# Hybrid decoder layer on one core: another order of the q, k, v preparation, the recurrence's norm in decode unit 0, query weights loaded later

## The reference

```python
h = rms_norm(x, norm1_g) * (1.0 + scale1) + shift1     # shift, scale, gate: silu(c) @ w_ada + b_ada
z = h @ w_in
x_lru, g_lru, q_lat, kv_lat, k_rope = split(z)          # 512, 512, 256, 128, 32 columns
x_conv = causal_dwconv(x_lru, ...)
hs = rg_lru(x_conv, ...)                                # h_t = a_t * h_(t-1) + u_t over the tokens
lru_out = hs * gelu(g_lru)
q = rms_norm(q_lat, q_lora_norm_g) @ w_uq               # 8 heads of 64 + 32
q_nope, q_rope = rms_norm(q[..., :64]), apply_rope(rms_norm(q[..., 64:]))
kv_lat = rms_norm(kv_lat, kv_lora_norm_g)
k_rope = apply_rope(rms_norm(k_rope, k_rope_norm_g))
attn = attend(q_nope, q_rope, kv_lat, k_rope)           # keys: rms_norm of kv_lat @ w_ukv, per head; values
mixed = concat([rms_norm(lru_out, lru_out_norm_g), rms_norm(attn, mla_out_norm_g)]) @ w_o
x = x + gate1 * mixed
x = x + gate2 * mlp(rms_norm(x, norm2_g) * (1.0 + scale2) + shift2)
```

## Time and profile before

| | us |
|---|---|
| median of 3 runs | 1013.28 |
| lowest and highest | 1012.67, 1016.78 |
| the profiled execution | 1014.83 |
| its span on the core | 1013.0 |

### The profile page before, as it was taken

The page is one execution under the profiler, slowest core; times in us unless marked ns, Lnnn a source line. Parts: engine busy times, 40 slices in busy tenths (PEclk is TensorE's granted clock), DMA queues, the critical chain, the costliest instruction groups (busy, mean ns, idle before and its releaser), DMA issues.

```text
span 1013.0 us, 20471 instructions
## 1 busy us (share of the span) xinstructions
PE 944.9 (93%) x7908; PEld 880.4 (87%) x7908; DVE 659.4 (65%) x1259; ACT 528.5 (52%) x1183; POOL 183.0 (18%) x186
## 2 busy tenths in 40 slices
PE   6599798889999999999988988999999999999997
PEld 3388675679999999999987988999999999999997
DVE  2694267538889879879783557777777777732321
ACT  2323553458898898988973333444434443321210
POOL 0021120322333343333210131000101001000000
PEclk9699899879999999999996998999999999999999
DMA  9965740600122022022101430333333331653202
GB/s 339 333 193 170 229 160 7 231 1 2 28 100 84 22 104 85 22 85 93 55 19 45 134 69 27 99 83 83 83 106 101 83 83 41 171 154 79 61 4 85
DMA packets 106289, 100.13 MB, mean 99 GB/s; under 512 B 7119, under 2 KB 94943, under 8 KB 104126
## 3 DMA queue, kind: packets, MB, share of 16 engines
q1 hardware_dynamic: 102422, 77.91, 26.4%
q0 software_dynamic: 3456, 20.97, 5.9%
q10 hardware_dynamic: 340, 0.27, 0.1%
HBM read 96.41 MB, written 2.94 MB: 98 GB/s over the span
## 4 chain that ended last, share of the span: by engine, by line
PE 85%; DVE 7%; ACT 3%; DMA 3%; issue 1%; SPq 0%; DVEq 0%; ACTq 0%
PE ps L874 50%; PE ps L1242 19%; PE ps L869 7%; DMA RW<-w_ada 3%; PE ps L900 2%; PE ps L1149 2%; PE ps L1200 1%; PE ps L1237 1%; PE ps L1175 1%; PE ps L1035 1%; DVE RB L1913 1%; DVE normed_low L1814 1%; DVE RB L1788 0%; DVE RB L2235 0%; PE ps L1100 0%
## 5 line engine op out<-in xcount | busy, mean ns | idle before, releaser
L874 PE MATMUL ps<-normed_high,up_weights_high 128*128 128x260 f32 x704 | 142.7, 284 | 3.4 <-DVE normed_low L1814 3.2
L874 PE MATMUL ps<-normed_high,up_weights_low 128*128 128x260 f32 x704 | 142.3, 284 | 0.0
L874 PE MATMUL ps<-normed_low,up_weights_high 128*128 128x260 f32 x704 | 142.1, 284 | 0.0
L1654 ACT ACTIVATE up_weights_high<-RW 128x1024 fp32r<-128x1024 f32 x44 | 46.6, 1061 | 137.2 <-PE ps L874 133.3
L1242 PE MATMUL ps<-key_weights_high,latents_high 128*128 128x260 f32 x528 | 117.4, 304 | 0.7 <-ACT RB L1596 0.6
L832 POOL TENSOR_TENSOR latents_low<-RB,latents_high 128x512 fp32r<-128x512 f32 (+1 forms) x72 | 86.2, 1198 | 174.8 <-ACT latents_high L1549 174.8
L874 PEld LDWEIGHTS ps<-normed_high,up_weights_high 128*128 128x128 f32 x704 | 109.2, 190 | 4.1 <-issue 3.3
L874 PEld LDWEIGHTS ps<-normed_high,up_weights_low 128*128 128x128 f32 x704 | 109.0, 189 | 0.0
L874 PEld LDWEIGHTS ps<-normed_low,up_weights_high 128*128 128x128 f32 x704 | 108.8, 189 | 0.0
L1242 PE MATMUL ps<-key_weights_low,latents_high 128*128 128x260 f32 x528 | 107.2, 285 | 0.0
L1242 PE MATMUL ps<-key_weights_high,latents_low 128*128 128x260 f32 x528 | 107.2, 285 | 0.0
(11 more groups left out here) (314 smaller groups left out, 2178.2 us busy)
## 6 DMA issues: line engine op xcount, KB each, us to landing
RW<-w_ada SPq DMA_DIRECT2D x24, 1024.0 KB, 8.6
RW<-w_up SPq DMA_DIRECT2D x44, 512.0 KB, 5.0
RW<-w_down SPq DMA_DIRECT2D x8, 1408.0 KB, 7.2
RW<-w_in SPq DMA_DIRECT2D x11, 512.0 KB, 8.0
RB<-w_o SPq DMA_DIRECT2D x8, 512.0 KB, 4.1
RB<-x_prompt SPq DMA_DIRECT2D x2, 1024.0 KB, 12.6
o_y_p<-RB SPq DMA_DIRECT2D x4, 512.0 KB
cst<-consts SPq DMA_DIRECT2D x1, 845.0 KB, 11.2
```

Source lines behind the costliest of these rows:

```text
L874: last = mm(ps[j % 4][rows[0]:rows[1], h, 0:H], lhsT, src[:, h * H:(h + 1) * H], start=start, stop=stop)
L1654: A(wuH[:, KT * g:KT * g + KT, :], wup[:, c, KT * g:KT * g + KT, :], ACT.Copy).then_inc(s_whi, 1)
```

## The change

Nothing is computed differently; the order changes, and with it the slots and some buffers.

- **TensorE.** kv0 and kv1 go ahead of w9, kv2 and kv3 behind it (before: behind w10 and w11). qst and qa go behind w10. The last w_ada chunk and c5 go ahead of w11. The norm sum of the recurrence (nlru) leaves the stretch: it is done in decode unit 0 behind key tile 5, as a job of the key slots.
- **ACT.** The recurrence's two Ln go ahead of the two latent norms, its Exp ahead of the gate branch. Squares and norms follow TensorE's order; query tiles go in pairs. The high part of the key weights is made here (before: DVE). The recurrence's squares and norm go into unit 0, behind key tiles 1 and 6.
- **DVE.** The recurrence goes ahead of the third group of modulation columns, the copy of modulation rows 4 and the rope key's norm. The copy of modulation rows 5 goes behind query tiles 2 and 3. The multiplication with the recurrence's norm (4 operations) goes into groups 2 and 3 of unit 0.
- **POOL.** It makes the low part of the key weights. Before its first latents_low it also waits for the ten output stores, because that buffer now lies on otok and lout, from which they are made.
- **SP.** The query and value weights are issued one projection chunk and one w_ada chunk later.

The diff, cut:

```diff
-            + ["gr", "wt", "w6", "r4", "nq", "w7", "c3", "nkv", "w8", "kr0", "w9", "r5", "qs", "kr1", "q0", "q1", "w10", "c4",
-               "q2", "q3", "kv0", "kv1", "w11"])
-PREP_ORDER = ["c5", "qst", "kv2", "kv3"] + [f"l{n}" for n in range(7)] + ["qa", "spread", "nlru"]
+            + ["gr", "wt", "w6", "r4", "nq", "w7", "c3", "nkv", "w8", "kr0", "kv0", "kv1", "w9", "r5", "kv2", "kv3", "qs", "kr1",
+               "q0", "q1", "w10", "c4", "qst", "qa", "q2", "q3", "c5", "w11"])
+PREP_ORDER = [f"l{n}" for n in range(7)] + ["spread"]
 
...
+J_NLRU = 2 + LRU_AT + 1
+KEY_JOBS = UNIT * NS + 1
...
-        latL = nc.alloc_sbuf_tensor_at("latents_low", [P, 3, 4 * P], FR, offset=rb_at + 4 * 11120)
+        latL = nc.alloc_sbuf_tensor_at("latents_low", [P, 3, 4 * P], FR, offset=behind_at)
...
-                if n == 8:
+                if n == 9:
                     query_weights()
...
+            pool.wait_ge(s_wkn, 16)
+            pool.wait_ge(s_kw, 2)
+            for e in range(2):
+                nc.gpsimd.tensor_tensor(kwL[:, e, :, 0:4 * NOPE], wk2, kwH[:, e, :, 0:4 * NOPE].bitcast(F32), ALU.subtract).then_inc(s_kw, 1)
...
+            pool.wait_ge(s_out, 16 * 10)
...
+            pe.wait_ge(s_kvn, 1)
+            pe.wait_ge(s_wq, 32)
+            keys_and_values(0)
+            keys_and_values(1)
+            w_in(9)
+            later_chunk(12)
+            later_chunk(13)
+
+            keys_and_values(2)
+            keys_and_values(3)
...
-            queries(2)
-            queries(3)
-            pe.wait_ge(s_kvn, 1)
-            keys_and_values(0)
-            keys_and_values(1)
-            w_in(11)
-            later_chunk(15)
-            mod_columns(5)
...
+            claim(pe, J_QA)
+            pe.wait_ge(s_qg, 4)
+            pe.wait_ge(psum_free[J_WT % 4], free_value(J_WT))
+            for h in range(HEADS):
+                last = mm(flat(J_QA)[:, NS * h:NS * h + NS], keyT[0:NOPE, P * h:P * h + P], gq8[:, h, :], start=True, stop=True)
+            last.then_inc(psum_full[J_QA % 4], 1)
...
+            queries(2)
+            queries(3)
+            later_chunk(15)
+            mod_columns(5)
+            w_in(11)
...
+            def lru_sum():
+
+                kclaim(J_NLRU)
+                for k in range(LT):
+                    pe.wait_ge(s_sq, KT + 4 + k + 1)
+                    for h in range(2):
+                        last = mm(kslot(J_NLRU)[:, h, 0:H], ones, lru_sq[:, k, h * H:(h + 1) * H], start=(k == 0), stop=(k == LT - 1))
+                last.then_inc(key_full[J_NLRU % 3], 1)
...
+            act.wait_ge(s_tiny, 1)
+            st.did(A(sq[:, 4:8, :], TA[:, :, :], ACT.Ln, bias=1.0))
+            st.seq(A(TA[:, :, :], TA[:, :, :], ACT.Ln))
+            act.sem_inc(s_lru, 1)
...
+            act.wait_ge(s_tiny, 2)
+            A(TA[:, :, :], TA[:, :, :], ACT.Exp, scale=0.5).then_inc(s_lru, 1)
...
+                        if u == 0 and (g, n) == (0, 1):
+                            lru_squares()
+                        if u == 0 and (g, n) == (1, 2):
+                            lru_rstd()
...
+            dve.wait_ge(s_lru, 1)
+            V.scalar_tensor_tensor(TA[:, :, :], TA[:, :, :], LN2, sq[:, 4:8, :], ADD, SUB).then_inc(s_tiny, 1)
...
+            mod_columns(3)
+            mod_rows(4)
+            dve.wait_ge(s_rs, 4)
+            R = (NOPE, QK)
+            kr = krT[NOPE:QK, :]
+            V.scalar_tensor_tensor(kr, kr, pr("gk", 0, 1, R), sq[NOPE:QK, 2, :], MUL, MUL).then_inc(s_kr, 1)
...
+            for a in range(2, 4):
+                prep_sums(5 + a, query_sq[a % 2], HEADS)
+            prep_query_tile(2)
+            prep_query_tile(3)
+            mod_rows(5)
+            dve.wait_ge(s_kr, 2)
+            dve.wait_ge(s_qtok, 4)
+            V.tensor_copy(headk[NOPE:QK, :], krT[NOPE:QK, 0:NP]).then_inc(s_krk, 1)
+            mod_columns(5)
...
+                        if u == 0 and g in (2, 3) and n % 2 == 1:
+                            lru_normed(2 * g + n // 2 - 4)
```

184 lines of the change are left out of this document (73 added, 111 removed).

## The result

The changed kernel takes 1028.18 us (median of 4 runs, 1027.41 to 1028.27), the kernel before 1014.15 (4 runs, 1012.67 to 1016.78): a ratio of 1.0134, with a 95% interval of 1.0111 to 1.0157. It is slower by 1.3%. I had forecast 1013.9, with a range of 1008.5 to 1019.7. The profiled execution took 1027.41 with a span of 1025.6, against 1014.83 and 1013.0 before, so these two executions differ by 12.6 us.

A forecast was written before the change was run, and what follows sets the result against it. TensorE, 85% of the span, was taken as the bound. Unit 0's first key product 3.7 us early and unit 0 4.3 longer gave +0.6 on the median 1013.28: 1013.9 us, range 1008.5 to 1019.7.

The forecast's parts named there:

- The 6.85 us and their half clock: TensorE's wait before the second modulation chunk goes, with the slow clock behind it; next projection chunk 9.0 us early.
- The waits at kr0 and c5: New TensorE waits for DVE: 7.9 us at the key-rope norm, 6.4 at the last modulation columns, each with 2.0 half clock.
- The waits at kr1 and qa: TensorE waits 1.6 us for DVE to finish keys 2, and 1.2 for the turned sample queries before the eight products.
- the first gain: Next projection chunk starts 9.0 us early at 112.9; nearly all handed back at the key-rope norm.
- preparation in the new order: TensorE's jobs from the key-rope norm on: queries 2 and 3 end at 178.5, the last projection chunk at 194.5.
- from there to K: Last projection chunk to unit 0's first key product: fetch 195.1, new-token row 209.1, that product 211.2, 3.7 us early.
- Rival (b): Stores pass only after the whole fetch drains: first key product of unit 0 at 217.0, time 1019.7 us; chance 0.18.
- the norm in unit 0: Decode unit 0 grows 4.3 us: products 2.8, DVE's multiplications 1.5, ACT's squares 0.
- Rival (a): Stores share with the fetch, row lands with the latents: unit 0's first key product at 209.3, time 1011.2 us; chance 0.20.
- the weight split: Key-weight copies move to ACT, subtractions to POOL; DVE loses 2.2 us of work; effect 0, up to 1.

The follow-up runs named there:

- the kernel of four repairs: Changed kernel with modulation columns ahead of scans, modulation rows ahead of query tiles 2 and 3, norm in fetch wait, unit-1 fetch behind new-token rows: 1004.90 us.

## Why the prediction was wrong

**Right.** The 6.85 us and their half clock go. The waits at kr0 and c5 come, each with its cause: undoing one order each brought back 10.2 and 5.3 us, forecast 9.9 and 8.4. The second is less for the most part because waits of 1.57 and 0.49 remained in the same place. The waits at kr1 and qa came at 1.60 and 1.18, forecast 1.6 and 1.2. That most of the first gain would be handed back was right, and it was the smaller half of the matter.

**Wrong, step "preparation in the new order" (6.0 us at the first fetch).** Two terms took TensorE to be at full clock where it was not. Behind the wait at kr0, which ended 0.7 late, the granted clock averaged 0.53 from 136.7 to 145, so keys 0 and 1 (1.7 each in the sum) came out at half clock for longer than the 2.0 us counted, and the chunk behind them began 2.4 late. (How long it lasts is in part chance: from kr0 to the next w_ada chunk eleven profiles with the same code and wait took 12.8 to 14.2 us, this one 14.2.) And queries 2 and 3 took 8.4, not 5.2: I had counted the wait of 1.2 at qa and not what stands at half clock behind it. The run with qa behind the tiles shows that term alone. The wait at c5 was 0.9 longer, as long as one addition of DVE was held up at 188.43 (last section). With 0.3 more for qa, c5 began 6.8 late; the last projection chunk was then 1.2 shorter than its sum, and the fetch began 0.5 later behind it: 6.0.

**Wrong, step "from there to K" (5.7 us).** The sum took stores and fetches as served in the order of issue, so that the row would land 14 behind the first fetch. It was used 19.2 behind. What the runs show in place of that order is sharing by packets: from 205 to 218 us 858 packets of the stores passed beside 710 of the fetch, and the row, last of its queue, came when both were through. In the kernel with the row ahead of the eight stores it was there within 7.6 us of its issue, in the middle of the fetch. I read the earlier trace rows the wrong way: no packet of the stores passed before 199, but the first of them was issued only at 195.65, and in the changed kernel too nearly 2 us lie between the issue at 203.21 and the first packets. The size of the fetch was wrong as well: it moved 5.24 MB for both units, and the sum has 3.1.

Rival (b) had K 21.9 behind the first fetch, and 21.8 was measured. That is luck as far as its reason goes: the stores didn't pass only when the fetch had drained, three quarters of their packets passed before.

**Mis-sized, the norm in unit 0 (4.3 forecast, 6.9 in the profile, 7.8 by the run with the norm outside).** The products were taken at 2.8 and the multiplications at 1.5, near enough to 3.3 and 1.7. What was left out is what goes on around them, 2 us: ACT has nothing to do while TensorE multiplies for the norm, and its Ln and Exp then stand ahead of the copies that TensorE needs, which shows as a wait of 0.72, and 1.2 is open; and the squares, set at 0, cost 0.9.

**What it did not see.** The frame of the sum, "K is set by the fetch and the row", was right, but it priced the new order only up to the fetch. Before, 23 us of TensorE's work (kv2, kv3, the transposes for output, qa, the norm) lay behind the last projection chunk and covered the fetch. The change moved kv2, kv3 and qa ahead of that chunk and the norm behind K, and left 8.4 us, so that TensorE waits 7.31 and 6.05 for transfers. The kernel with the norm in that wait has unit 0 7.8 us shorter and K no later; the kernel with the last chunk ahead of queries 2 and 3 gives cover back, loses the wait at c5 and is 14 us faster.

Rival (a), that the stores share with the fetch, had the reason nearly right and the time wrong (K 14.2 behind the first fetch): it let the row land as soon as the latents, and left out that more than a thousand small packets stand ahead of the row in its queue. The Trainium skill, DMA: Bandwidth & Descriptors, "Queues, rings and completion order", has each engine go round its queues a packet at a time. The trace agrees, if what it counts as packets are those of the rule: 96 of q1 passed beside 118 of q0 from 214 to 216, 0.02 MB against 0.81, in 4.7% of the engines' time.

Of the weight split, which the sum put at nothing, the subtractions on POOL held up one addition of DVE by 1.0 us (last section); what the copies on ACT cost was not run by itself.

## What to carry to other kernels

Price a reordering at the next transfer that it must wait for, by what TensorE still has to do while that transfer runs, and not only by the waits ahead of it: here the work that was moved, ahead of the last projection chunk and behind K, was the cover of a fetch. A small wait is worth its length and the half clock of what stands behind it, and an inserted step in a tight pipeline costs its own time and the bubble of every engine that it starves. When repairs that each worked don't add up, look first for an instruction that was queued behind a moved one on its engine; two memsets of 0.1 us were worth 5.3 us at the head of unit 1 here. And a small transfer that the next step needs goes ahead of large ones in its queue, with a look at every other wait that ends with that queue.

## What the runs showed of the hardware

**One port for two engines.** DVE's addition of two SBUF operands took 1.38 us beside POOL's subtraction and 0.42 without it. From DVE's timeline of the changed kernel, and POOL's row of the same moment:

```profile
188.43 1.38 DVE L1995 TENSOR_TENSOR sq<-FS,UT 128x256 f32<-128x256 f32 x1
...
191.75 0.42 DVE L1995 TENSOR_TENSOR sq<-FS,UT 128x256 f32<-128x256 f32 x1
```

```profile
188.27 2.67 POOL L793 TENSOR_TENSOR key_weights_low<-wkn,key_weights_high 128x512 fp32r<-128x512 f32 x2 [33.27 <-ACT key_weights_high L1531]
```

That is 1.0 us on the chain to c5, where the prediction gave the Trainium skill's rule (SBUF — State Buffer, "SBUF: two separate sides") up to 2.6 and left it out of the sum. The rule holds here, at less than half of that bound. The four multiplications in the kernel of four repairs show it again: 4.78 us beside POOL's latents_low, where the shortest in the changed kernel takes 0.75, which makes 3.0 for four.

**The same code at another clock.** From the head of the last prompt head's unit to the end no kernel here changes anything, yet the profiled executions take 521.1 us there (after), 522.8 (before) and 524.9 (qa behind the queries). The difference shows in the out-projection, behind a stretch in which TensorE is busy for less than half (3.5 of the 10 us from 540.5 in the changed kernel). Windows of 10 us, 50 us behind that head, of after, before, and of the kernel with qa behind the queries (window, us, busy times, granted clock, DMA share, GB/s):

```profile
554.49:564.49 10.00, 8.82 (x73) 8.15 (x65) 1.68 (x5) 2.22 (x4) 0.00 (x0) 0.83 0.39 107
```

```profile
540.23:550.23 10.00, 9.35 (x72) 8.54 (x65) 1.81 (x5) 2.22 (x4) 0.00 (x0) 0.67 0.40 107
```

```profile
549.54:559.54 10.00, 9.35 (x63) 8.62 (x56) 1.72 (x5) 0.85 (x2) 0.00 (x0) 0.50 0.39 107
```

The clock returns to 2.4 GHz at another moment in each. I did not find what sets it. It explains 1.7 of the 2.3 us by which 14.9 at the head of unit 1 became 12.6 at the end (0.6 went in the units between), and it is a reason to compare profiles at a mark inside the kernel and not by their spans when a few microseconds matter.
